# A routed decoder trunk on one core: eight turns in TensorE's visit loop, one weight rest moved, and an ordered last down-projection

## The reference

```python
logits = xf @ w_router
top_vals, top_idx = top_k(logits, 2)
gates = softmax(top_vals)
# per token: sum over its two experts of gate * (silu(x @ w1[e]) * (x @ w3[e])) @ w2[e]
```

## Time and profile before

| | |
|---|---|
| median of 3 runs | 2067.91 us (2066.62 to 2069.62) |
| the profiled execution | 2069.79 us, its span 2068.1 us |
| TensorE busy | 2014.9 us, 97% |
| VectorE, ScalarE busy | 1539.8 us, 1202.7 us |
| mean granted clock | 0.99 of 2.4 GHz |

### The profile page before, as it was taken

How to read it: one execution, slowest core, us unless ns; L and a number is a source line. 1 busy time by engine, 2 the same in 40 slices (tenths; PEclk the granted TensorE clock), 3 DMA queues, 4 the chain that set the end, 5 groups by cost and what they waited for, 6 DMA issues and landing times.

```text
span 2068.1 us, 33621 instructions
## 1 busy us (share of the span) xinstructions
PE 2014.9 (97%) x11091; PEld 1748.2 (85%) x11092; DVE 1539.8 (74%) x1705; ACT 1202.7 (58%) x1546; POOL 96.7 (5%) x142
## 2 busy tenths in 40 slices
PE   8999999999999998999999999999999999999996
PEld 7777888888888777999899988888999888889995
DVE  6896766666668976766577688898776798997774
ACT  4443555555555333655465577787655687876661
POOL 1000000100000002100000000000000000001010
PEclk9999999999999998999999999999999999999998
DMA  7321776766643313877587699999877799999771
GB/s 223 120 72 47 223 219 202 218 197 190 185 143 123 112 71 103 275 236 234 204 273 253 196 360 377 357 394 353 288 254 245 278 388 357 388 356 360 258 254 41
DMA packets 245272, 487.51 MB, mean 236 GB/s; under 512 B 16724, under 2 KB 86468, under 8 KB 245220
## 3 DMA queue, kind: packets, MB, share of 16 engines
q1 hardware_dynamic: 237668, 462.04, 66.1%
q0 software_dynamic: 7552, 24.80, 3.4%
HBM read 473.21 MB, written 13.58 MB: 235 GB/s over the span
## 4 chain that ended last, share of the span: by engine, by line
PE 82%; DVE 9%; issue 3%; DMA 3%; ACT 2%; POOL 0%; DVEq 0%; SPq 0%; ACTq 0%; POOLq 0%
PE PS L1575 81%; DMA raw<-in_expert_w 2%; DVE PS L894 2%; DVE wlo L753 2%; ACT whi L375 1%; DVE OV L868 1%; DVE OV L882 1%; PE PS L1903 1%; PE PS L1605 0%; DVE OV L898 0%; DVE OV L864 0%; PE PS L1827 0%; DMA OV<-in_norm_mix_g 0%; DMA OV<-x_tok,idx 0%; DMA raw<-in_w_in 0%
## 5 line engine op out<-in xcount | busy, mean ns | idle before, releaser
L753 DVE TENSOR_TENSOR wlo<-raw,whi 128x1024 fp32r<-128x1024 f32 x872 | 1031.9, 1221 | 201.8 <-ACT whi L375 195.9
L375 ACT ACTIVATE whi<-raw 128x1024 fp32r<-128x1024 f32 x872 | 888.0, 1053 | 255.5 <-PE PS L1575 155.9
L1575 PE MATMUL PS<-XN,whi 128*128 128x512 f32 (+3 forms) x3328 | 953.5, 363 | 15.1 <-issue 9.7
L1575 PE MATMUL PS<-XN,wlo 128*128 128x152 f32 (+3 forms) x2944 | 775.3, 263 | 1.0 <-issue 1.0
L1575 PEld LDWEIGHTS PS<-XN,whi 128*128 128x128 f32 x3328 | 618.7, 189 | 81.6 <-issue 17.5
L1575 PE MATMUL PS<-whi,XN 128*128 128x512 f32 x2272 | 672.5, 394 | 7.1 <-issue 2.2
L1575 PEld LDWEIGHTS PS<-XN,wlo 128*128 128x128 f32 x2944 | 561.9, 191 | 12.8
L1575 PEld LDWEIGHTS PS<-whi,XN 128*128 128x128 f32 x2272 | 424.5, 188 | 102.3 <-issue 6.9
L1575 PE MATMUL PS<-wlo,XN 128*128 128x512 f32 x1248 | 425.0, 392 | 0.0
L1575 PEld LDWEIGHTS PS<-wlo,XN 128*128 128x128 f32 x1248 | 234.7, 188 | 50.8
L587 ACT ACTIVATE OV<-PS 128x352 f32<-128x352 f32 x112 | 51.5, 461 | 107.8 <-PE PS L1575 107.8
(11 more groups left out here) (248 smaller groups left out, 991.6 us busy)
## 6 DMA issues: line engine op xcount, KB each, us to landing
raw<-in_expert_w SPq DMA_DIRECT2D x672, 512.0 KB, 5.1
raw<-in_ffn_w SPq DMA_DIRECT2D x144, 512.0 KB, 3.8
raw<-in_w_in SPq DMA_DIRECT2D x40, 512.0 KB, 5.4
raw<-in_w_out SPq DMA_DIRECT2D x16, 512.0 KB, 4.3
y_rows<-OV POOLq DMA_DIRECT2D x13, 512.0 KB, 4.8
y_rows<-OV POOLq DMA_DIRECT2D x13, 192.0 KB, 5.1
RES<-in_x SPq DMA_DIRECT2D x4, 512.0 KB, 5.5
x_tok<-OV POOLq DMA_DIRECT2D x4, 512.0 KB, 2.9
```

The costliest lines, as they stand in the source:

```text
L375: act.activation(whi[:, u0 % CONV, half(h)], raw[:, r, half(h)], ACT.Copy).then_inc(s["hi_done"], 1)
L753: dve.tensor_tensor(wlo[:, w, half(h)], raw[:, u0 % RAW, half(h)], whi[:, w, half(h)].bitcast(F32), ALU.subtract).then_inc(s["lo_done"], 1)
L1575: return pe.matmul(out_, lhsT, rhs, start=start, stop=stop, skip_group_check=True)
```

## The change

TensorE's loop has eight turns. The first transposes and the wait for `sizes` stand ahead of it, `turn` and the entry and absent classes are gone. After the loop TensorE reads the number of further windows: with none, it goes on with `to_tokens`; otherwise further visits and the last expert follow in code of their own. The sizes are computed ahead of the table of further windows. VectorE makes the rest of unit 3 ahead of the transposed rows' rests, and that of unit 4 inside the first visit, at its start when light, between the first and the second sum when heavy. All heavy visits end with `heavy_end`: first the extension's products of all four tiles, then the top rows', those of the last unit by halves. The last visit's copies and rests follow in that order, and `to_tokens` takes the extension first. The last token block is scaled and stored in two halves.

```diff
@@ first visits, last window (lines 249, 271)
-                c = eng.value_load(sizes[0:1, bass.ds(v + 1, 1)], min_val=0, max_val=2)
+                c = eng.value_load(sizes[0:1, bass.ds(v, 1)], min_val=0, max_val=2)
@@ sync, store of the blocks (line 356)
-                sp.wait_ge(s["fin_ready"], b + 1)
-                sp.dma_start(out[0, b * P:(b + 1) * P, :], RES[:, b, :]).then_inc(s["out_done"], 16)
+                for h in range(1 if b < TB - 1 else 2):
+                    sp.wait_ge(s["fin_ready"], b + 1 + h)
+                    c = slice(512 * h, 512 * h + 512) if b == TB - 1 else slice(0, D)
+                    sp.dma_start(out[0, b * P:(b + 1) * P, c], RES[:, b, c]).then_inc(s["out_done"], 16)
@@ scalar, last_visit (line 676)
+                act.wait_ge(s["y_ext"], i + 1)
+                for h in range(2):
+                    act.activation(yExt[:, h, :], PS[:, 6 + h, :], ACT.Copy).then_inc(s["ty_hi"], 1)
+                act.wait_ge(s["y_top"], i + 1)
+                act.activation(yTop[:, 0, :], PS[:, 4, :], ACT.Copy).then_inc(s["ty_hi"], 1)
                 act.wait_ge(s["unit_used"], i * UNITS + (CONV + UNITS))
-                for part, first in ((yTop, 4), (yExt, 6)):
-                    for h in range(2):
-                        act.activation(part[:, h, :], PS[:, first + h, :], ACT.Copy).then_inc(s["ty_hi"], 1)
+                act.activation(yTop[:, 1, :], PS[:, 5, :], ACT.Copy).then_inc(s["ty_hi"], 1)
@@ vector, heavy (line 1084); light calls lead() at its start
                 heavy_sum(i, 0, 0, (0,))
+                if lead:
+                    lead()
                 m_split(i, 0, 5)
                 heavy_sum(i, 0, 0, (1,))
@@ vector, after the scan of the counts (line 1302)
+            step(dve.tensor_scalar(further, cum[:, E - 1:E], 0.0, 4.0, ALU.is_gt, ALU.mult))
+            step(dve.tensor_copy(classes[:, E:E + 1], classes[:, E - 1:E]))
+            step(dve.tensor_tensor(classes[:, E - 1:E], classes[:, E - 1:E], further, ALU.max))
+            dve.tensor_copy(sizes[0:1, 0:E + 1], classes[0:1, 0:E + 1]).then_inc(s["sizes_ok"], 1)
+            split(MOE_BASE + 3, 0)
+            dve.wait_ge(s["sizes_ok"], 1)
+            x_split(0)
+            x_split_ext(0)
             ... (the table, as before; the old sizes, with six steps and three copies, and x_split go)
@@ vector, ahead of the visits (line 1350)
-            for i in range(3, LEAD):
-                split(MOE_BASE + i, 0)
-            first_windows(dve, visit)
+            def first_visit(v, c):
+                def lead():
+                    with dve.If(v < 1):
+                        split(MOE_BASE + 4, 0)
+                    with dve.Else():
+                        dve.nop()
+                visit(v, c, lead)
+            first_windows(dve, first_visit)
@@ tensor, new; called at the end of heavy instead of m_down(i, 0, UNITS - 2, ...)
+            def heavy_end(i):
+                for t in range(4):
+                    u = MOE_BASE + UNITS - 2 + t // 2
+                    pe.wait_ge(s["lo_done"], i * (2 * UNITS) + (2 * u + t % 2 + 1))
+                    for ws in (whi, wlo):
+                        for h in range(2):
+                            a = (t % 2) * D + h * GROUP
+                            ins = mm(PS[:, 6 + h, :], hidE3[:, t, :], ws[:, u % CONV, a:a + GROUP], False,
+                                     t == 3 and ws is wlo)
+                ins.then_inc(s["y_ext"], 1)
+                for q, halves in ((0, ((0, 1),)), (1, ((0,), (1,)))):
+                    w = (MOE_BASE + UNITS - 2 + q) % CONV
+                    for hh in halves:
+                        for j in range(2):
+                            for hs, ws in ((hidH3, whi), (hidH3, wlo), (hidL3, whi)):
+                                for h in hh:
+                                    a = j * D + h * GROUP
+                                    ins = mm(PS[:, 4 + h, :], hs[:, 2 * q + j, :], ws[:, w, a:a + GROUP], False,
+                                             q == 1 and j == 1 and hs is hidL3)
+                        if hh[-1]:
+                            ins.then_inc(s["unit_used"], 1)
+                        else:
+                            ins.then_inc(s["y_top"], 1)
@@ tensor, the loop (line 2012)
-            pe.wait_ge(s["entry_ok"], 3)
             keep_busy(2, 4)
-            with pe.Fori(0, VIS + 1) as v:
+            gT(0)
+            gT_ext()
+            pe.wait_ge(s["sizes_ok"], 1)
+            with pe.Fori(0, E) as v:
                 c = pe.value_load(sizes[0:1, bass.ds(v, 1)], min_val=0, max_val=4)
                 with pe.If(c > 2):
+                    pe.nop()
+                with pe.Else():
+                    with pe.If(c > 0):
+                        heavy(v, c)
+                    with pe.Else():
+                        light(v)
+            n_more = pe.value_load(table[0:1, 7:8], min_val=0, max_val=MORE)
+            with pe.If(n_more < 1):
+                rows_to_tokens()
+            with pe.Else():
+                ... (further visits heavy(.., WIDE), then the last expert and rows_to_tokens)
```

More of the change, by code:

```diff
@@ L1049, in light_group, with light @@
                 m_split(i, g, 7, 8)
-            def light(i, ends=(5, 6), between=None):
+            def light(i, ends=(5, 6), between=None, lead=None):
+                if lead:
+                    lead()
                 m_split(i, 0, 5, 6)
@@ L1082, in heavy_group, with heavy @@
                 heavy_sum(i, g, 1)
-            def heavy(i, ends=(5, 6), between=None):
+            def heavy(i, ends=(5, 6), between=None, lead=None):
                 heavy_sum(i, 0, 0, (0,))
+                if lead:
+                    lead()
                 m_split(i, 0, 5)
@@ L1101, in heavy, with visit @@
                 heavy_lo(i, GROUPS - 1, 1)
-            def visit(i, c):
+            def visit(i, c, lead=None):
                 ext = c is not None
                 if ext:
-                    heavy(i)
+                    heavy(i, lead=lead)
                 else:
-                    light(i)
+                    light(i, lead=lead)
                 x_split(i + 1)
@@ L1170, in last_lo @@
             def last_lo():
-                for n, (part, low_part, first) in enumerate(((yTop, yTopLo, 4), (yExt, yExtLo, 6))):
+                for n, (part, low_part, first) in enumerate(((yExt, yExtLo, 6), (yTop, yTopLo, 4))):
                     for h in range(2):
@@ L1960, in to_tokens @@
                 cols = slice(b * P, b * P + P)
+                hi, low = ((yExt, yExtLo), (yTop, yTopLo))[n]
                 for h in range(2):
-                    for part, first in (((yTop, yTopLo), (yExt, yExtLo))[n][0], True), (((yTop, yTopLo), (yExt, yExtLo))[n][1], False):
+                    for part, done in ((hi, "ty_hi"), (low, "ty_lo")):
                         if b == 0:
-                            pe.wait_ge(s["ty_hi" if first else "ty_lo"], 2 * n + h + 1)
-                        ins = mm(PS[:, 2 * b + h, :], maps[:, n, cols], part[:, h, :], n == 0 and first,
-                                 n == 1 and not first)
+                            pe.wait_ge(s[done], 2 * n + h + 1)
+                        ins = mm(PS[:, 2 * b + h, :], maps[:, 1 - n, cols], part[:, h, :], n == 0 and part is hi,
+                                 n == 1 and part is low)
                 if n:
@@ L2018, in _ @@
+            with pe.If(n_more < 1):
+                rows_to_tokens()
+            with pe.Else():
+                with pe.Fori(0, MORE) as j:
+                    with pe.If(j < n_more):
+                        heavy(j + (E - 1), WIDE)
+                    with pe.Else():
                         pe.nop()
[L2019 to L2022 removed]
+                c = pe.value_load(sizes[0:1, E:E + 1], min_val=0, max_val=2)
+                with pe.If(c > 0):
+                    heavy(n_more + (E - 1), c)
@@ L2023, in _ @@
                 with pe.Else():
-                    i = pe.value_load(turn[0:1, bass.ds(v, 1)], min_val=0, max_val=VIS - 1)
-                    with pe.If(c > 0):
-                        heavy(i, c)
-                    with pe.Else():
-                        light(i)
-            pe.wait_ge(s["map_ok"], 2)
-            to_tokens(0, 0)
-            to_tokens(1, 0)
-            to_tokens(0, 1)
-            to_tokens(1, 1)
-            for b in (2, 3):
-                to_tokens(b, 0)
-                to_tokens(b, 1)
+                    light(n_more + (E - 1))
```

57 lines of the change are left out of this document (23 added, 34 removed).

## The result

The changed kernel takes 2056.20 us (median of 5 runs, 2053.67 to 2058.25) against 2067.91 (median of 5, 2065.83 to 2069.62) for the kernel before on the same chip. The ratio is 0.9944, with an interval of 0.9933 to 0.9955. It is 11.7 us faster; 8.7 were forecast (2059.2).

What follows compares the result with a forecast made beforehand. TensorE, busy 97% of the span, was taken as the bound, with savings in its idle stretches: tail 7.5, entry 0.5, border 0.7, together 8.7 us off, giving 2059.2 us; range 2055.5 to 2063.3.

Steps and rivals of the forecast that it cites:

- a tail bound by the sequencer: After the last visit: TensorE's sequencer needs 8.1 us for five absent turns, leaving 4.64 us of TensorE idle.
- an entry jump that goes: Before visit 0: the 3.58 us branch out of the entry turn disappears; first product about 3.35 us earlier.
- Tail: After the last visit to the end: 7.5 us saved, bounds 6 to 8.5.
- The step that put 0.4 us on the smaller transfer and 0.15 against it: Last store in halves: smaller last transfer saves 0.4 us, scaling in two halves costs about 0.15 us.
- The third rival: Tail: rows-to-tokens code, first met inside a branch, must be fetched; 2060.5 to 2066, typically 2062.2; chance 0.12.
- TensorE's other far jump: After TensorE's last product: jump over the other outcome costs nothing, beside 10 us of VectorE.
- Entry: Up to and in visit 0: 2.6 us gained minus 2.1 us waiting for VectorE's second sum, 0.5 net, bounds -0.4 to 3.
- Border: Between visits 0 and 1: 6.08 us branch stays, clock still falls, gap 3.9 us; 0.7 us saved, bounds 0.5 to 3.4.
- rival 1: Clock does not fall between visits 0 and 1, or rises earlier at entry: 2.7 us more, 2056.5; chance 0.12.
- The prediction's ground for free later borders: Borders after visit 0: at light to heavy, 1435.6, one product follows the other with no gap.
- the 0.7 us of the turn's read: Between visits 0 and 1: only the read of the turn goes, 1008.1 to 1008.8, saving 0.7 us.
- Rivals 2 and 4: 2: later release starves light visits, 2064.6, chance 0.09. 4: loop not resident, jumps after visits 1, 4 cost 13.2 us, 2072.4, 0.05.

Runs made afterwards that it cites:

- e12: The kernel before, run again unchanged for a second trace; 2067.16 us.
- e1: The kernel before with nine loop turns instead of fourteen, so without the five absent turns; 2062.07 us, ratio 0.9975.
- e2: The kernel before with only the last products, copies and rests in the changed kernel's order; 2066.41 us, ratio 0.9999.
- e8: The changed kernel with the last token block scaled and stored whole instead of in halves, one run; 2059.13 us.
- e3: The changed kernel, run again unchanged for a second trace; 2055.63 us, ratio 0.9944.
- e4: The changed kernel with the rest of unit 4 made ahead of the first visit again; 2057.40 us, ratio 0.9952.
- e11: The changed kernel with 256 filler semaphore increments on TensorE ahead of the visits, shifting its later code; 2076.84 us, ratio 1.0045.
- e9: The changed kernel with 172 filler semaphore increments on TensorE ahead of the visits, shifting its later code; 2062.75 us, ratio 0.9979.
- e5: The changed kernel with the light body ahead of the heavy body in TensorE's loop; 2060.30 us, ratio 0.9967.
- e10: The changed kernel with 172 filler semaphore increments on TensorE and the rest of unit 4 ahead of the first visit; 2060.07 us, ratio 0.9962.

## Why the prediction was nearly right

The two readings that carry the forecast, a tail bound by the sequencer and an entry jump that goes, held. That the total came out near is partly luck: the entry's misses cancel and the border's adds.

**Tail: right, 7.75 us for 7.5.** (Of the sequencer's time there, 3.85 us were hidden, not the 4.0 of the prediction: 2038.2 to 2042.05.) The issue gap goes, TensorE's 32 products follow at once, the clock stays full, and VectorE's chain is the bound from its first sum on. The first sum gains 10.21 - 2.83 = 7.4 us (7.2 forecast); the rest from there to the end goes from 15.87 to 15.50, but e12, e1 and e2 have 15.56, 15.51 and 15.50 with the store as before, so it belongs to none of the edits to the store. The step that put 0.4 us on the smaller transfer and 0.15 against it was wrong, both small: the last issue comes 0.12 us later after the first sum than in e8, and the end of the span 0.13 us sooner after that issue. The third rival was wrong for the path taken. TensorE's other far jump, over the second outcome after its last product, did take 3.3 us from 2037.9 and hid behind VectorE as the prediction said.

**Entry: the net near, both parts too small.** First product at 808.73 (809.35 forecast), the clock full from 808.0 on, so 3.7 us are gained from the transposes on where I took 2.6. Against them stands a cost of 3.9 instead of 2.1. The wait for the sum is there as forecast, 1.73 us (0.2 before). Not foreseen were the issue gap's growth from 0.97 to 2.21 us, and that the clock falls behind each of the two gaps (3.4 us at half each, so up to 1.7 lost each). Before, 4.4 us of visit 0 ran at half clock, a loss of up to 2.2. The sum is 1.5 + 1.2 + 1.2 = 3.9. So this entry is worth -0.2 us in the pair of traces, or 0.1 with the 0.3 us ahead of the transposes, where 0.5 were forecast: two misses that cancel. The clock differs between executions of the same kernel: half for the first 4.3 us of visit 0 and full behind both gaps in e3, half behind the second gap alone in e8.

**The issue gap.** The first product behind it is always the 143rd of visit 0 (after, e3, e4, e8, e11), 140th before the change (before, e12, e1, e2). The first group has 128 products, so by the program it is the 15th behind the branch over the body of 152 columns (12th before), with as many weight loads some 30 instructions. The "64 instructions" of the expectations count the rows that start later than the branch's; about half of these stand ahead of the branch in the program and were only executed later. The argument of e9 needs the shift alone, so it stays. The Trainium skill, "Runtime: NRT & Kernel Launch", section "Instruction fetch mechanics", says that code is fetched in blocks of 256 instructions, one after the other, and that a branch breaks this. The trace agrees: 29 instruction packets of 0.48 MB in all are some 16.5 KB each, one of them moves from 831.65 to 832.69, and a shift by 256 restores the gap. I read it so that the fetch of the block behind the landing begins too late for some 30 instructions to cover it. When it is asked for is not shown: the branch ends at 827.93, and the packet starts 3.7 us later, in e3, e4, e8 and e11 3.7 to 4.5, with the old code (before, e12, e1, e2) 2.3 to 2.5. I had the rule at hand and applied it only to the branches themselves, not to what follows a landing.

**Border: the step that failed.** The prediction kept the branch at 6.08 us and let the clock fall. The branch took 4.38, 4.44, 4.38 and 4.92 in four traces with the changed kernel's TensorE program (after, e3, e8, e4), and 6.08, 5.43, 4.48 and 5.10 in four with the old head (before, e12, e1, e2). So a single trace had shown me its longest case. The gap was 2.15, 2.22, 2.16 and 2.79 us where 3.9 were forecast. The clock fell in e3 and e4 and did not in the other two. That it doesn't fall is rival 1, whose 2056.5 is near the measured time, reached half by its mechanism and half by a shorter branch. The prediction's ground for free later borders, was a border behind a light visit, where no light body is jumped over; borders behind heavy visits bear it out (the branch at 1190.7 took 0.21 us). With the 0.7 us of the turn's read, which did go, the border is worth 2.5 us in gap in this pair of traces, 1.7 of it the shorter branch, and in two of four traces 2 to 3 us of clock.

The packet records say where the branch's length varies. In all 14 traces it ends 1.2 to 1.5 us after the end of its last instruction packet, and the packet mostly takes 0.9 to 1.4 us. What differs is how long after the branch's start the packet starts: 2.0, 2.1, 2.0 and 2.6 us in after, e3, e8 and e4, and 3.6, 3.1, 2.1 and 2.7 in before, e12, e1 and e2. For the branch behind the last product, when no weights move, it is 0.9 to 1.1 us in all traces that have it.

**The rest.** Between visit 1 and the end 4.7 us are saved in the traces. About 2.6 are the clock at visit 1's start. Of the remaining 2.1 us, 1.7 lie in visit 4, where a wait for VectorE's sum in the second group comes and goes between executions: near 1457 to 1463 us none (after), 1.55 (before), 2.69 (e3), 1.90 (e10). Visit 7 has one at times, 1.72 in e8. Such waits are part of why the traces differ by more than the medians. Rivals 2 and 4 were wrong: the light visits take 121.6 us as before, from first product to first product, and no issue gap stands at a border after the first. A window over visit 2 of the changed kernel, to be read beside the earlier trace rows:

```profile
1179.00:1302.00 123.00, 122.75 (x553) 1.00 0.98 357
```

**What stays open.** Why the packet of the border's branch starts after 2.0 to 3.6 us, whether the difference between the old and the new code is layout or chance, and why in e5 a target that had run already was fetched again. Also whether the kernel would be faster without the gap near 832. And no run changes the entry alone: that its 4.1 us come from the jump that went is read from the traces, not tested.

## What to carry to other kernels

An idle stretch that the profile calls "issue" is to be read on the sequencer's rows: what ran there, how far ahead of the array it began, and so how much of it is bare. Remove the sequencer's lateness before ordering the data; the order alone was worth nothing here (e2), behind it 1.7 us. A branch over a large body can cost twice, at the branch and again a few dozen instructions behind the landing, where a shift of the code may remove the second. The size of either must come from several executions, not one. Nor does the sum of the stretches of one pair of traces show what each edit is worth: here the middle of the kernel varied by 4 us between executions of the same code.

## What the runs showed of the hardware

- **Far branches.** A far branch that had to fetch took 3.3 us with nearly idle DMA queues (2037.9; 3.3 to 3.8 in the other traces) and up to 6.4 beside weight transfers (e5). It ended 1.2 to 1.5 us behind its packet's end in each case. In the changed kernel no packet of the queue that TensorE's stalls go with (q8) moves from 1012 to 2037 us, over seven visits and some 1450 instructions of loop (counted from the code). The same section of the Trainium skill gives TensorE room for 2048 instructions, which agrees, and elsewhere a window of two blocks, which here doesn't. The prediction had used the latter.
- **Clock.** Behind the border's gap it stayed at 2.4 GHz after 2.15 us (after), 2.16 (e8) and 2.41 (e10), and fell to 1.2 after 2.09 (e9), 2.11 (e11), 2.22 (e3) and 2.79 (e4). After 1.73 us in visit 0 it fell in after and did not in e3, e8 and e9.
- **Stores.** 256 KB and 512 KB both take 2.6 to 2.7 us from issue to landing.
- **Fillers.** A semaphore increment is 51 ns on TensorE's sequencer. With 172 of them the stages ahead of the visits took 10.6 us longer (e9) or 7.9 (e10), with 256 of them 20.2 (e11). Of that the clock at half, for 10.2, 6.8 and 17.1 us of these stages, is up to 5.1, 3.4 and 8.5 us; the rest is 26 to 46 ns an increment. So they are not free even in busy stretches.
